# Mixture of experts in fp32: down of expert e-1 after gate and up of expert e, 512-column gate/up units, low halves in place and shared by two engines

## The reference

```
logits = h @ w_router + b_router            # 512 x 32
top_w, top_idx = softmax(top 4 of logits)   # each token goes to 4 of 32 experts
# tokens grouped by expert, groups padded to blocks of 128 rows
gu = x_block @ w_gate_up[e] + b_gate_up[e]  # 1024 x 2048
a  = min(gate, 7) * sigmoid(1.702 * min(gate, 7)) * (clip(up, -7, 7) + 1)
y  = a @ w_down[e] + b_down[e]              # 1024 x 1024
out[token] += weight * y
```

## Time and profile before

| | |
|---|---|
| three executions | 2059.5, 2063.12, 2069.91 us |
| profiled execution | its span from first to last instruction is 2065.3 us; no other time of it was taken |
| PE busy | 1740.7 us, 84% |
| DVE, ACT, POOL busy | 67%, 55%, 36% |
| moved by DMA | 495.48 MB, mean 240 GB/s |
| mean granted clock of PE | 0.922 |

### The profile page before, as it was taken

One profiled execution on the slowest core, in us unless ns is written; L12 is line 12 of the kernel. 1 busy time (PEld: TensorE's weight loads), 2 busy tenths in 40 slices (PEclk: granted clock), 3 DMA queues, 4 the chain that ended last, 5 costly groups with the idle time before them and its releaser, 6 DMA issues.

```text
span 2065.3 us, 27412 instructions
## 1 busy us (share of the span) xinstructions
PE 1740.7 (84%) x7534; PEld 1324.2 (64%) x7535; DVE 1375.5 (67%) x1327; ACT 1138.8 (55%) x1162; POOL 749.4 (36%) x438
## 2 busy tenths in 40 slices
PE   6999966781699988989899989898899989889880
PEld 1788844441577766767677767676777767767760
DVE  0444469433678887548888888864688888655865
ACT  2322244410577766557677767763677767635740
POOL 2000000103344555325444554543345554433541
PEclk9999975995799999999999999999999999999995
DMA  7665330113699999558999899974699999846956
GB/s 228 229 218 201 102 115 0 34 75 103 215 309 319 320 315 306 177 189 302 319 316 320 297 321 314 329 264 150 235 314 315 309 323 317 303 142 219 303 182 244
DMA packets 380689, 495.48 MB, mean 240 GB/s; under 512 B 21052, under 2 KB 284312, under 8 KB 380050
## 3 DMA queue, kind: packets, MB, share of 16 engines
q1 hardware_dynamic: 363456, 458.27, 65.7%
q0 software_dynamic: 14592, 34.72, 4.9%
q10 hardware_dynamic: 2610, 2.11, 0.3%
HBM read 490.75 MB, written 27.09 MB: 251 GB/s over the span
## 4 chain that ended last, share of the span: by engine, by line
PE 52%; issue 12%; DVE 9%; POOL 3%; DMA 2%; ACT 2%; DVEq 0%; POOLq 0%; SPq 0%; ACTq 0%
PE ps L993 14%; PE ps L994 14%; PE ps L995 14%; DVE wl L1108 4%; PE ps L622 3%; PE ps L942 2%; PE ps L989 2%; POOL gsu L1231 1%; DVE gsu L1139 1%; DVE gsu L1143 1%; PE ps L954 1%; DMA yt<-expert_rows 1%; DMA rawm<-in_w_gate_up 1%; POOL slot_rows L803 1%; ACT wh L1022 1%
## 5 line engine op out<-in xcount | busy, mean ns | idle before, releaser
L1108 DVE TENSOR_TENSOR wl<-rawm,wh 128x2048 fp32r<-128x2048 f32 x320 | 778.2, 2447 | 129.7 <-ACT wh L1022 129.4
L1022 ACT ACTIVATE wh<-rawm 128x2048 fp32r<-128x2048 f32 x384 | 730.4, 1912 | 164.4 <-PE ps L995 107.9
L993 PE MATMUL ps<-wh,xh 128*128 128x512 f32 x1120 | 471.2, 421 | 23.9 <-POOL wl L1236 23.9
L994 PE MATMUL ps<-wl,xh 128*128 128x512 f32 x1120 | 440.0, 393 | 0.0
L995 PE MATMUL ps<-wh,xl 128*128 128x512 f32 x1120 | 439.9, 393 | 0.0
L1231 POOL TENSOR_TENSOR gsu<-gsu 128x256 f32<-128x256 f32 x140 | 208.2, 1487 | 433.2 <-DVE gsu L1143 389.9
L1236 POOL TENSOR_TENSOR wl<-rawm,wh 128x2048 fp32r<-128x2048 f32 x64 | 342.6, 5354 | 15.6 <-ACT wh L1022 15.6
L993 PEld LDWEIGHTS ps<-wh,xh 128*128 128x128 f32 x1120 | 213.8, 191 | 74.2 <-issue 34.9
L993 PE MATMUL ps<-wh,ah 128*128 128x512 f32 x560 | 247.7, 442 | 0.0
L995 PEld LDWEIGHTS ps<-wh,xl 128*128 128x128 f32 x1120 | 212.2, 189 | 46.3
L994 PEld LDWEIGHTS ps<-wl,xh 128*128 128x128 f32 x1120 | 213.0, 190 | 42.5
(11 more groups left out here) (233 smaller groups left out, 2054.8 us busy)
## 6 DMA issues: line engine op xcount, KB each, us to landing
rawm<-in_w_gate_up SPq DMA_DIRECT2D x512, 512.0 KB, 5.0
rawm<-in_w_down SPq DMA_DIRECT2D x128, 1024.0 KB, 5.1
raw<-in_w_ada SPq DMA_DIRECT2D x24, 1024.0 KB, 5.4
raw<-in_w_in SPq DMA_DIRECT2D x16, 1024.0 KB, 5.2
yt<-expert_rows POOLq DMA_DIRECT2D x4, 2048.0 KB, 9.3
wo<-in_w_out SPq DMA_DIRECT2D x2, 2048.0 KB, 17.5
bias_vectors_repeated<-bias_vectors POOLq DMA_DIRECT2D x1, 2304.0 KB, 15.7
xs<-in_x ACTq DMA_DIRECT2D x1, 2048.0 KB, 25.2
```

What stands on the lines that cost most here:

```text
L993: nc.tensor.matmul(dst, a_h[:, b, kk, :], wh[:, v % SPL, k, :], start=False, stop=False)
L994: nc.tensor.matmul(dst, a_h[:, b, kk, :], wl[:, v % SPL, k, :], start=False, stop=False)
L1022: nc.scalar.activation(flat(wh[:, v % SPL, :, :]), flat(rawm[:, v % RAW, :, :]), ACT.Copy).then_inc(wh_done, 1)
L1108: nc.vector.tensor_tensor(flat(wl[:, v % SPL, :, :]), flat(rawm[:, v % RAW, :, :]), flat(wh[:, v % SPL, :, :]), ALU.subtract).then_inc(wl_ ...
```

## The change

- Order. The loop is unrolled by hand (`passes`): body e does the 8 gate/up halves of expert e, then the token transposes of e+1, then the 4 down halves of expert e-1, then the transposes of e's activation, all 8 at once. The first body has no down halves, and the down halves of the last expert follow the last body.
- Units. A gate/up unit is 512 columns, gate (halves 0, 1 and 4, 5) and up (2, 3 and 6, 7) apart; each half is one DMA. Clamped gate, sigmoid and product are made for 512 columns; the sigmoid goes to PSUM bank 7, and DVE does all products (POOL's line 1231 goes).
- Buffers. There are 8 slots for raw halves, and the low part is written over the raw half in its slot. A slot is free when PE has used the half. `wh` keeps 4 slots. Activations lie in `actv`, 1024 columns per block; their transposes use the PSUM banks of the token transposes (5 and 6).
- Low split. DVE makes chunks 0 to 2 of every half, POOL chunk 3 (`LOW_K = 3`). PE waits for both.
- Gather and scatter. Tokens and outputs of block 0 share one buffer (`xy[0]`). POOL scatters the outputs of e-2 after its first split in body e, and gathers the tokens of e+1 after the fourth, once the scatter has landed.
- End. In the final sum, the residual rows share the semaphore of the expert rows.

The core of the diff:

```diff
-RAW, SPL = 4, 4
-POOL_LOW = (7, 11)
+RAW, SPL = 8, 4
+LOW_K = 3
...
-    wh = at("wh", [P, SPL, HK, UN], F32R, 32 * KB)
-    wl = at("wl", [P, SPL, HK, UN], F32R, 64 * KB)
+    wl = at("wl", [P, RAW, HK, UN], F32R, 0)
+    wh = at("wh", [P, SPL, HK, UN], F32R, 64 * KB)
...
+    def passes(eng, body):
+
+        body(0, Place(0, 0), False)
+        with eng.Fori(0, E // 2 - 1) as k:
+            body(2 * k + 1, Place(3 * k + 1, 0), True)
+            body(2 * k + 2, Place(3 * k + 2, 4), True)
+        k = E // 2 - 1
+        body(E - 1, Place(3 * k + 1, 0), True)
...
+        def load(place, v, src, free=True):
+            if free:
+                sp.wait_ge(half_used, place.count(v) - RAW)
+            sp.dma_start(rawm[:, place.slot(v), :, :], src).then_inc(rawm_in[place.slot(v)], 16)
...
+        def body(e, place, has_d):          # PE
             x = Expert(pe, e)
-            for v in range(9):
-                half(x, v)
-                if v in (3, 5, 7):
-                    act_transposed(x, (v - 3) // 2)
-            act_transposed(x, 3)
-            tokens_transposed(Expert(pe, e + 1))
-            for v in range(9, HALVES):
-                half(x, v)
+            before = Expert(pe, e - 1) if has_d else None
+            for v in range(N_GU):
+                gate_up_half_used(x, before, place, v)
+            last = is_last(e)
+            if not last:
+                tokens_transposed(Expert(pe, e + 1), e + 1)
+            if has_d:
+                for d in range(N_D):
+                    down_half_used(before, x, place, N_GU + d, d)
+            act_transposed(x, last)
...
+        def body(e, place, has_d):          # DVE
             x = Expert(dve, e)
+            before = Expert(dve, e - 1) if has_d else None
+            if has_d:
+                act_low(before, before.further)
+            for v in range(N_GU + N_D if has_d else N_GU):
+                if v in (1, 5):
+                    gate(x, v // 4, place, v)
+                if v in (3, 7):
+                    up(x, v // 4, place, v)
+                if v == 8 and not is_last(e):
+                    tokens_low(Expert(dve, e + 1))
+                if v in (2, 6):
+                    gate_done(x, v // 4, x.further)
+                split_low(place, v + SPL)
+                if v in (2, 6):
+                    gate_done(x, v // 4, at_once)
+                if v == 0 and has_d:
+                    act_low(before, at_once)
+            if not has_d:
+                tokens_low(Expert(dve, e + 1))
...
+        def split_low(place, v):            # POOL
+            pool.wait_ge(wh_done, place.count(v))
+            nc.gpsimd.tensor_tensor(flat(wl[:, place.slot(v), LOW_K:HK, :]), flat(rawm[:, place.slot(v), LOW_K:HK, :]),
+                                    flat(wh[:, place.split(v), LOW_K:HK, :]), ALU.subtract).then_inc(wl_pool_done, 1)
...
+        def body(e, place, has_d):
+            for v in range(N_GU + N_D if has_d else N_GU):
+                split_low(place, v + SPL)
+                if v == 0 and has_d and not (isinstance(e, int) and e < 2):
+                    stored_before(e)
+                if v == 3 and not is_last(e):
+                    gather(Expert(pool, e + 1), Expert(pool, e - 1) if has_d else None)
```

More of the change, by code:

```diff
@@ L908, in experts_sync, with tokens_transposed @@
             sp.wait_ge(h2_out[w], 32)
[L910 to L925, removed]
+        def load(place, v, src, free=True):
[4 more added lines that the diff above has]
+            for v in range(N_GU):
+                if not has_d and v == 6:
+                    sp.wait_ge(lg_ps, TC)
+                load(place, v, gate_up_half(e, v), free=has_d)
+            if has_d:
+                for d in range(N_D):
+                    load(place, N_GU + d, down_half(e - 1, d))
+        passes(sp, body)
+        for d in range(N_D):
+            load(LAST, d, down_half(E - 1, d))
     def experts_pe(pe):
         pe.wait_ge(nk_ready, 1)
-        def tokens_transposed(x):
+        def tokens_transposed(x, e):
+            if not (isinstance(e, int) and e == 0):
+                pe.wait_ge(al_done[0], e - 1 + START)
             def work(b):
@@ L1015, in experts_act @@
+        passes(pe, body)
+        end = Expert(pe, E - 1)
+        for d in range(N_D):
+            down_half_used(end, None, LAST, d, d)
     def experts_act(act):
         act.wait_ge(nk_ready, 1)
-        def split_high(x, v, used=None):
-            act.wait_ge(rawm_in[v % RAW], loaded(x.e, v))
-            if used is not None:
-                act.wait_ge(half_used, used)
-            nc.scalar.activation(flat(wh[:, v % SPL, :, :]), flat(rawm[:, v % RAW, :, :]), ACT.Copy).then_inc(wh_done, 1)
+        act.wait_ge(lg_ps, TC)
@@ L1024, in tokens_high, with split_high @@
+        def split_high(place, v, first=False):
+            act.wait_ge(rawm_in[place.slot(v)], place.arrivals(v))
+            if not first:
+                act.wait_ge(half_used, place.count(v) - SPL)
+            nc.scalar.activation(flat(wh[:, place.split(v), :, :]), flat(rawm[:, place.slot(v), :, :]),
+                                 ACT.Copy).then_inc(wh_done, 1)
         def tokens_high(x):
@@ new lines, in body @@
+            after = None
+            if has_d:
+                act_high(before, before.further)
+            for v in range(N_GU + N_D if has_d else N_GU):
+                split_high(place, v + SPL)
+                if v == 0 and has_d:
+                    act_high(before, at_once)
+                if v in (1, 5):
+                    sigmoid(x, v // 4)
+                if v == 7 and not is_last(e):
+                    after = Expert(act, e + 1)
+                    tokens_high(after)
+                if v in (9, 11):
+                    outputs(before, v // 2 - 4, place, v, after)
@@ new lines, in experts_act @@
+        passes(act, body)
+        end = Expert(act, E - 1)
+        act_high(end, end.blocks)
+        outputs(end, 0, LAST, 1, None)
+        outputs(end, 1, LAST, 3, None)
+    def experts_dve(dve):
+        def split_low(place, v):
+            dve.wait_ge(wh_done, place.count(v))
+            nc.vector.tensor_tensor(flat(wl[:, place.slot(v), 0:LOW_K, :]), flat(rawm[:, place.slot(v), 0:LOW_K, :]),
+                                    flat(wh[:, place.split(v), 0:LOW_K, :]), ALU.subtract).then_inc(wl_done, 1)
@@ L1179, in experts_pool @@
         pool.wait_ge(lg_ready, TC)
-        nc.gpsimd.memset(xg0[:], 0.0).then_inc(pool_set, 1)
-        for b in range(1, NB):
+        for b in range(NB):
             nc.gpsimd.memset(xy[b][:], 0.0).then_inc(pool_set, 1)
@@ new lines, in experts_pool, with body @@
+        first = Expert(pool, 0)
+        gather(first, None)
+        for v in range(SPL):
+            split_low(Place(0, 0), v)
+        def body(e, place, has_d):
+            for v in range(N_GU + N_D if has_d else N_GU):
+                split_low(place, v + SPL)
[3 more added lines that the diff above has]
+                    gather(Expert(pool, e + 1), Expert(pool, e - 1) if has_d else None)
```

387 lines of the change are left out of this document (188 added, 199 removed).

## The result

The changed kernel takes 2153.5 us (median of four executions, 2152.0 to 2160.1), beside 2066.5 us for the kernel before (median of four, one of them at 2136.3): a ratio of 1.042, 95% interval 1.040 to 1.045. It is slower by 87 us. Forecast was 1977 us, in a range of 1912 to 2045, with a chance of 0.09 on slower. The profiled execution has a span of 2150.3 us. From its page: busy time by engine, the clock that was granted (beside the earlier trace rows), the two queues that bring instructions, and the two parts of the low split.

What follows compares the result with a forecast made beforehand. PE's own chain was taken as the bound: 36.0 us arithmetic, about 2.4 gather wait and 0.6 clock made 39.0 us laps. Thirty laps, three additional blocks, start and end gave 1977 us, range 1912 to 2045.

Steps and rivals of the forecast that it cites:

- ordinary laps: One expert's full round on PE: 36.0 us arithmetic, about 2.4 gather wait, 0.6 clock; 39.0 us each.
- three bodies with two blocks: Experts with two token blocks: each additional block was to cost 46 us, three of them 138.
- from the last token transposes to the last multiplication: The last body and expert on PE: remaining halves, transposes and 2.7 us exposed before the last down halves.
- final part: After PE's last multiplication, storing the last rows and the final sum were to keep their 58 us.
- the register loads' too: they now stand behind queued multiplications, as the loop's own load does today: PE's waits behind register loads, 1.3 us on average per ordinary interval, were to go.
- The port: Path shared by DVE and POOL for low splits and products: taking turns, 34.5 to 36 us per expert.
- in lockstep: Slower rival: DVE's PSUM work not covered beside POOL's turns; lap 44.3 us, total 2136 us; chance 0.09.
- both serial chains: An additional block's tokens and activation, each through ACT's copy, DVE's split and semaphores in turn: 5.6 us.
- the 2.5 us of the earlier trace: PE's wait before the activation's transposes was to go, as four down halves of 11.4 us cover it.
- the gather's wait: PE waiting for the next expert's gathered tokens after half 7: about 2.4 us per lap, 0 to 5.
- The DMA bound: Moving 13.0 MB per expert at 349 GB/s: no lap under 37.3 us.
- The port rule: Skill's rule that the DVE-POOL port is an exclusive lock for a whole instruction; weighed, used for the slower rival.

Runs made afterwards that it cites:

- a1: The changed kernel without the never-executed code for a third and fourth block of tokens: 2075.0 us, ratio 1.003 to the kernel before.
- a2: The changed kernel with its loop written for one expert per turn and six raw slots instead of eight: 2058.6 us, ratio 0.996 to the kernel before.
- b2: The kernel before with two experts in each loop turn on all engines, nothing else changed: 2176.5 us, ratio 1.051.
- c1: The changed kernel with a one-expert loop, six raw slots and the whole low split on DVE: 2026.8 us, ratio 0.979 to the kernel before.
- d1: The changed kernel, two-expert loop kept, with the whole low split on DVE: 2111.7 us, ratio 1.021 to the kernel before.
- d3: The changed kernel with one-expert loop, six slots, DVE-only low splits, separate block-0 token buffer with earlier gather, tokens split first, separate residual semaphore: 1944.0 us.
- d2: The changed kernel with one-expert loop, six slots, DVE-only low splits and tokens split first, block 0's tokens and outputs sharing a buffer: 2016.3 us, ratio 0.975.

## Why the prediction was wrong

The miss, 2150.3 - 1979 = 171 us of the profiled execution, by the prediction's own terms (laps measured between the starts of PE's token transposes, 594.3 to 2016.2):

| term | forecast | measured | miss |
|---|---|---|---|
| 20 ordinary laps | 39.0 each | 42.9 each | 77 |
| three bodies with two blocks, each with its two successors | 163 (3 x 39 + 46) | 188.3, 188.7, 187.7 | 76 |
| up to the transposes in the first body with down halves | 589.1 (566.8 + 22.3) | 594.3 | 5 |
| from the last token transposes to the last multiplication | 62.4 (20 halves, 57.0, 2.7, and three times 0.9) | 73.3 | 11 |
| final part | 58.4 (2065.3 - 2006.9) | 60.8 | 2 |

**The step that failed: "the register loads' too: they now stand behind queued multiplications, as the loop's own load does today".** It was carried over from the loads to the jump, where the earlier trace rows shows 0.23 us for a loop of 1512 instructions. The diff doubles the loop; the prediction never counted its instructions and put the jump at nothing. It measured 4.3 us at the median of 14 jumps, with the clock often halved behind them. Of the 87 us of slowdown and the 176 us of the miss, 78 (a1) to 95 us (a2, which changes the slots too) are this; b2 shows it without anything else of the change. Of the 95, 54 are PE's gaps between an activation's transposes and the next bias (69.9 us over the stage against 15.9 in a2, 7 of each in the last expert), and about 34 are time at the halved clock (72.5 against 38.6). This step alone is not the whole miss: with it mended the kernel is level with the one before (2075.0 in a1, 2058.6 in a2) and still above the range's end of 2045. With POOL's splits gone as well it is inside (2026.8, c1).

**The port was mis-sized**: the sum of engine time was about right, the manner in which the two engines meet was not. The prediction let DVE and POOL take turns, split by split. The earlier trace rows had shown POOL behind DVE and DVE behind POOL once each, never two instructions of POOL in a row; the changed kernel makes them in threes. c1 and d1 put it at 32 and 42 us. The rival "in lockstep" had nearly the right time, 2136, by luck: it had DVE at 44.3 us of engine time per lap, and the windows show 37.7 and 38.2, its stalls included. (Its 6.4 us of PSUM work add up to 6.7 by its own terms.) DVE is not the bound; its splits come late because they are held up at the wrong time.

**Bodies with two blocks: estimated 5.6 us for both serial chains, measured 9.7 for the tokens and 4.5 for the activation** (medians of three). The sum counted the copy and the split of the tokens, and not what stands ahead of them in ACT's and DVE's order nor how long the port stretches it. In the changed kernel:

```profile
805.24 1.09 PE L967 MATMUL ps<-ident,xy 128*128 128x128 f32 x8 [1.38 <-DMA xy<-h_ffn,icur]
815.84 1.97 PE L967 MATMUL ps<-ident,xy 128*128 128x128 f32 x8 [9.51 <-DVE xl L1169]
```

With DVE free of POOL this idle time is 4.0 to 6.4 us (c1), with the tokens first as well 3.4 to 4.7 (d3). The activation's gap stayed in c1 (4.6 us of idle time), so it is not the port's; what makes it longer than forecast is open. The clock's loss is about 9.8 us in a body with two blocks and its two successors, where 3.3 was forecast; PE is idle up to 9.8 us at once in them.

**The end: 2.7 us exposed, measured 7.2.** Here too the order on DVE was left out: the low part of the last activation waits behind DVE's splits for the last down halves. PE, then DVE:

```profile
2068.96 1.04 PE L981 MATMUL ps<-ident,actv 128*128 128x128 f32 x8
2076.95 0.61 PE L995 MATMUL ps<-bparts,sel 96*128 96x512 bf16 x1 [6.95 <-DVE al L1177]
```

```profile
2065.71 10.04 DVE L1162 TENSOR_TENSOR wl<-rawm,wh 128x1536 fp32r<-128x1536 f32 x4
2075.68 1.21 DVE L1177 TENSOR_TENSOR al<-ps,ah 128x1024 fp32r<-128x1024 f32 x1
```

In d3, without POOL's splits, 5.2 us of this idle time are left.

**The final part was called unchanged** and lost 2 us. DVE's first product now waits for the residual too, and d3 gives 3 us back in the profiled execution, though not beyond the scatter of the medians:

```profile
2105.02 0.75 DVE L1363 TENSOR_SCALAR yo<-yt,topw 128x1024 f32<-128x1024 f32 x1 [28.13 <-DMA x1e<-x_after_mixing]
```

**What held.** No PE idle remains before the activation's transposes in a body with one block: the 2.5 us of the earlier trace rows are gone. Without the stall at the jump the lap is 39.4 us (a2) against the forecast 39.0. This nearness is luck, for the parts are others: 0.9 of gather, not 2.4, and 2.1 of waits between multiplications and before biases, mostly for late low splits, not none. Once the splits no longer held PE, the gather's wait was 1.6 to 1.9 (d2, c1). The gathers from 560 us on landed 0.4 us later than forecast, 7.1 for 6.7:

```profile
DMA to landing us min/median/max: 6.0/7.1/9.2
```

The DMA bound did not hold: 37.3 us per lap came from a stretch at 349 GB/s, and laps of 35.9 at 363 GB/s followed (d3). The wider slices left fewer packets (363,456 before, 228,288 after); the prediction took no gain from that, and no run here separates the rate from the width. The port rule that the prediction weighed was a better guide than my reading of the earlier trace rows. The Trainium skill (SBUF — State Buffer, "SBUF: two separate sides") says that the lock is exclusive and the loser fully blocks, for one instruction. The trace agrees, and goes further: 5.20 us beside three splits of POOL's shows that even at the ends of the first two the loser didn't come in.

What the new order itself is worth, beside the kernel before with DVE alone splitting (2002.2): with one expert to a turn and the tokens split first it is 14 us slower with one buffer for tokens and outputs (2016.3, d2) and 58 us faster with two (1944.0, d3).

## What to carry to other kernels

Count the instructions in a loop before doubling it, those behind branches that never run included, and look at the instruction queue in the profile: packets in every turn say that the loop is loaded anew, and here PE, with the longest body, paid at the jump. Don't give a small share of a critical operation to an engine that shares the port and comes in bursts; one line that took POOL out of the splits was worth more than the whole reordering as written. For each operation in a serial chain, write down what stands ahead of it on its own engine, not only its duration.

## What the runs showed of the hardware

- Code that is never executed can cost time: 78 us (a1), by making the loop longer (2957 instructions of PE, not 1509).
- A loop of 1512 instructions of PE stayed loaded (2 packets from 560 us on), one of 2957 was loaded anew in each turn (200 packets), with 4.3 us at each jump.
- Splits of POOL in immediate succession kept DVE out for all three (5.20 us for an operation of 1.75); 91 of DVE's 384 splits took over 1.5 times the median of 1.76.
- Moving a third more columns onto DVE left the mean of its split where it was (2.26 us in a2, 2.29 in c1); none of the 384 splits of c1 took longer than 2.3 us.
- Weights in rows of 2 KB came at 363 GB/s on average over a whole lap (d3), beside 315 with gate and up in rows of 1 KB, where PE's waits set the rate.
